# Convolution taps shared anew between VectorE (in PSUM) and TensorE, and seven norms in column form

## The reference

```python
def rmsnorm(x, g):
    y = x * lax.rsqrt(jnp.mean(x * x, axis=-1, keepdims=True) + EPS)
    return y * g

def conformer_conv_module(u, w_pw1, b_pw1, dw_w, dw_b, ln_g, ln_b, w_pw2, b_pw2):
    h = u @ w_pw1 + b_pw1                       # 1024 -> 2048
    a, g = jnp.split(h, 2, axis=-1)
    h = a * jax.nn.sigmoid(g)
    h = causal_depthwise_conv(h, dw_w, dw_b)    # 31 taps per channel
    h = jax.nn.silu(layernorm(h, ln_g, ln_b))
    return h @ w_pw2 + b_pw2
```

## Time and profile before

| | |
|---|---|
| median of 3 runs | 3100.71 us (3097.72 to 3105.9) |
| profiled execution, its own time | 3102.5 us |
| its span, first to last instruction | 3100.7 us |
| mean granted TensorE clock | 0.918 |
| busy: PE, DVE, ACT, POOL | 89%, 48%, 34%, 35% |
| stretch of the convolution taps | 2448.8 to 2644.0 us |
| norms with a reciprocal of 128 x 512 ahead of the product | n0, n1, n2, n3, n4, n6, n8 |

### The profile page before, as it was taken

How to read it: one execution, slowest core, us unless ns; L and a number is a source line. 1 busy time by engine, 2 the same in 40 slices (tenths; PEclk the granted TensorE clock), 3 DMA queues, 4 the chain that set the end, 5 groups by cost and what they waited for, 6 DMA issues and landing times.

```text
span 3100.7 us, 34247 instructions
## 1 busy us (share of the span) xinstructions
PE 2766.6 (89%) x12475; PEld 2225.4 (72%) x12475; DVE 1487.5 (48%) x2187; ACT 1050.2 (34%) x1661; POOL 1100.6 (35%) x551
## 2 busy tenths in 40 slices
PE   3985689899998888999989999999999867799997
PEld 2764457777787667888878888788888644588886
DVE  7499772555414773322133566433321599533312
ACT  2221532322223573333223555433322200433321
POOL 1321001334443222445424455444444322144442
PEclk6897657999999998999979999999999988899998
DMA  6431040355423101223221221122223210122221
GB/s 212 136 109 55 1 136 28 102 161 163 139 95 86 41 28 55 95 95 100 93 61 60 69 64 60 67 95 97 95 92 99 82 41 27 41 95 95 95 95 55
DMA packets 277692, 264.47 MB, mean 85 GB/s; under 512 B 23020, under 2 KB 276557, under 8 KB 277581
## 3 DMA queue, kind: packets, MB, share of 16 engines
q1 hardware_dynamic: 277581, 262.97, 26.6%
HBM read 260.85 MB, written 2.10 MB: 85 GB/s over the span
## 4 chain that ended last, share of the span: by engine, by line
PE 66%; DVE 19%; issue 7%; ACT 2%; DMA 2%; POOL 2%; SPq 1%; DVEq 0%; POOLq 0%; ACTq 0%
PE bank L1153 16%; PE bank L1155 16%; PE bank L1154 16%; DVE v_cm L2182 6%; DVE ada_acc L2347 2%; POOL w_lo L805 2%; DMA root<-in_ada_w_dram 2%; PE bank L893 1%; PE bank L895 1%; PE bank L894 1%; PE bank L1491 1%; DVE root L2353 1%; DVE score L2530 1%; PE bank L1422 1%; PE bank L915 1%
## 5 line engine op out<-in xcount | busy, mean ns | idle before, releaser
L805 POOL TENSOR_TENSOR w_lo<-w_raw,w_hi 128x1024 fp32r<-128x1024 f32 (+1 forms) x364 | 867.7, 2393 | 1651.9 <-ACT w_hi L1740 1079.8
L1153 PE MATMUL bank<-h_hi,w_hi 128*128 128x512 f32 x1632 | 650.6, 399 | 75.7 <-DVE u_pad L2189 30.3
L1154 PE MATMUL bank<-h_lo,w_hi 128*128 128x512 f32 x1632 | 645.0, 395 | 0.0
L1155 PE MATMUL bank<-h_hi,w_lo 128*128 128x512 f32 x1632 | 644.3, 395 | 0.0
L1740 ACT ACTIVATE w_hi<-w_raw 128x1024 fp32r<-128x1024 f32 (+1 forms) x232 | 232.6, 1015 | 588.2 <-PE bank L1155 514.9
L1153 PEld LDWEIGHTS bank<-h_hi,w_hi 128*128 128x128 f32 x1632 | 312.8, 192 | 148.2 <-issue 47.6
L1154 PEld LDWEIGHTS bank<-h_lo,w_hi 128*128 128x128 f32 x1632 | 313.1, 192 | 66.4 <-issue 1.2
L1155 PEld LDWEIGHTS bank<-h_hi,w_lo 128*128 128x128 f32 x1632 | 312.5, 191 | 67.1
L1153 PE MATMUL bank<-a_hi,w_hi 128*128 128x512 f32 x704 | 273.9, 389 | 0.0
L1154 PE MATMUL bank<-a_lo,w_hi 128*128 128x512 f32 x704 | 273.9, 389 | 0.0
L1155 PE MATMUL bank<-a_hi,w_lo 128*128 128x512 f32 x704 | 273.9, 389 | 0.0
(11 more groups left out here) (343 smaller groups left out, 4596.0 us busy)
## 6 DMA issues: line engine op xcount, KB each, us to landing
ada_w<-in_ada_w_dram SPq DMA_DIRECT2D x60, 512.0 KB, 6.0
w_raw<-in_ffn_gate_dram SPq DMA_DIRECT2D x22, 1024.0 KB, 5.1
w_raw<-in_ffn_up_dram SPq DMA_DIRECT2D x22, 1024.0 KB, 5.2
w_raw<-in_ffn_w_gate_dram SPq DMA_DIRECT2D x22, 1024.0 KB, 5.2
w_raw<-in_ffn_w_up_dram SPq DMA_DIRECT2D x22, 1024.0 KB, 5.1
root<-in_ada_w_dram SPq DMA_DIRECT2D x144, 128.0 KB, 2.8
w_raw<-in_ffn_down_dram SPq DMA_DIRECT2D x16, 1024.0 KB, 5.1
w_raw<-in_ssm_w_in_dram SPq DMA_DIRECT2D x16, 1024.0 KB, 5.2
```

Source lines behind the costliest of these rows:

```text
L805: pool.tensor_tensor(w_lo[parity][:, 0:nk, half], w_raw[parity][:, 0:nk, half], w_hi[parity][:, 0:nk, half].bitcast(F32), ALU.subtract).th ...
L1153: pe.matmul(dst[m][:], hi, src_hi(k0 + k), start=first and k == 0, stop=False)
L1154: pe.matmul(dst[m][:], hi, src_lo(k0 + k), start=False, stop=False)
L1155: ins = pe.matmul(dst[m][:], lo, src_hi(k0 + k), start=False, stop=last and k == nk - 1)
```

## The change

- `PE_TAPS` becomes a list by chunk, 9, 9, 9, 9, 9, 10, 14, 15: 84 taps on PE instead of 64.
- `own_taps` accumulates in PSUM bank 5 instead of `v_cm`; the last tap writes `v_cm`.
- DVE's order: the `u_pad` of the next pair come between the two chunks of a pair instead of behind them.
- The diagonals go from POOL (`root`) to ACT (`tap_diag`, two buffers of 16), one activation of 128 x 128 for each tap; ACT does those of chunks c and c+1 behind the sigmoid of each odd c.
- The mean's products (`mean_part`) are spread between slots and taps on PE.
- Norms n0 to n4, n6 and n8: the sums are made with the data as the stationary operand and one column of ones as the moving one, so that bank 4 holds 128 x 4 numbers; the root and the reciprocal work on 128 x 4 (`norm_col`); `spread` on PE multiplies the broadcast column by the identity, so that the factor stands in all rows of bank 4 again, and DVE reads it there in L2309.

```diff
@@ constants and buffers
-PE_TAPS = 8
+PE_TAPS = [9, 9, 9, 9, 9, 10, 14, 15]
+        norm_col = place("norm_col", [P, NT])
+        tap_diag = [in_big(f"tap_diag{j}", [P, 16, P], 72 + 8 * j) for j in range(2)]
@@ gpsimd: tap_diagonals(c) and its calls at m = 3..9 are taken out
@@ cv_pe
             def conv_taps(c):
                 pe.wait_ge(glu_done, c + 1)
-                pe.wait_ge(diag_ready, 2 * c + 2)
+                pe.wait_ge(diag_ready, c + 1)
                 take(6 + c % 2, taps_done, c + 1)
-                for k in range(PE_TAPS):
-                    ins = pe.matmul(bank[6 + c % 2][:], root[k // 4][:, P * (k % 4):P * (k % 4) + P], u_pad[:, c, k:k + S],
+                for k in range(PE_TAPS[c]):
+                    ins = pe.matmul(bank[6 + c % 2][:], tap_diag[c % 2][:, k, :], u_pad[:, c, k:k + S],
...
+            def mean_part(c):
+                if c == 0:
+                    take(4, centred, DC)
+                pe.wait_ge(taps_done, c + 1)
+                ins = pe.matmul(bank[4][:], ones[:], v_cm[:, c, :], start=c == 0, stop=c == DC - 1)
...
                     if 2 * j + q >= 2:
                         conv_taps(2 * j + q - 2)
+                    if 2 * j + q >= 5:
+                        mean_part(2 * j + q - 5)
             conv_taps(6)
+            mean_part(3)
             conv_taps(7)
-            (mean of all 8 chunks here)
+            for c in range(4, DC):
+                mean_part(c)
@@ norm_sums, spread (called behind every norm_sums but those of norms 5 and 7)
                 pe.wait_ge(x_squared, DC * nn + DC)
-                pe.matmul(bank[4][:], ones[:], sq[1][:], start=False, stop=True).then_inc(x_sq_summed, 1)
+                for i in range(NT):
+                    tok = slice(P * i, P * i + P)
+                    pe.matmul(bank[4][:, i:i + 1], tmp[0][:, tok], ones[:, 0:1], start=True, stop=False)
+                    ins = pe.matmul(bank[4][:, i:i + 1], sq[1][:, tok], ones[:, 0:1], start=False, stop=True)
+                ins.then_inc(x_sq_summed, 1)
+            def spread(nn):
+                pe.wait_ge(rinv_ready, ROOT_BASE[f"n{nn}"] + 1)
+                take(4, h_scaled, H_BASE[nn] + DC)
+                for i in range(NT):
+                    ins = pe.matmul(bank[4][:, P * i:P * i + P], norm_col[:, i:i + 1].to_broadcast([P, P]), ident[:],
+                                    start=True, stop=True)
+                ins.then_inc(rinv_spread, 1)
@@ scalar: rms writes norm_col from bank[4][:, 0:NT]; in the convolution stage
+                def diagonals(c):
+                    if c >= 2:
+                        act.wait_ge(pe_taps_done, c - 1)
+                    for k in range(PE_TAPS[c]):
+                        ins = act.activation(tap_diag[c % 2][:, k, :], ident[:], ACT.Copy, scale=col("dw_w", DC * k + c))
+                    ins.then_inc(diag_ready, 1)
+                diagonals(0)
...
+                    if c % 2 == 1:
+                        diagonals(c)
+                        if c + 1 < DC:
+                            diagonals(c + 1)
@@ cv_dve
+                k0 = PE_TAPS[c]
+                acc = bank[5]
+                link(dve.tensor_scalar(acc[:], u_pad[:, c, k0:k0 + S], tap(k0), col("cv_dw_b", c), ALU.mult, ALU.add))
+                for k in range(k0 + 1, TAPS):
+                    link(dve.scalar_tensor_tensor(out=acc[:] if k < TAPS - 1 else v, in0=u_pad[:, c, k:k + S], scalar=tap(k),
+                                                  in1=acc[:], op0=ALU.mult, op1=ALU.add))
...
+            glu_pair(0)
+            for j in range(DC // 2):
+                own_taps(2 * j)
+                if j + 1 < DC // 2:
+                    glu_pair(j + 1)
+                own_taps(2 * j + 1)
@@ vector
+            def rinv_cols(nn):
+                dve.wait_ge(root_done, r + 1)
+                dve.reciprocal(norm_col[:], norm_col[:]).then_inc(rinv_ready, 1)
+                dve.wait_ge(rinv_spread, SPREAD[nn] + 1)
+                return bank[4]
```

More of the change, by code:

```diff
@@ L298, in build @@
         rinv_ready = sem("rinv_ready")
+        rinv_spread = sem("rinv_spread")
         h_scaled = sem("h_scaled")
@@ L806, in low_part @@
                                        w_hi[parity][:, 0:nk, half].bitcast(F32), ALU.subtract).then_inc(w_split, 1)
[L808 to L815, removed]
             n = 0
@@ L1242, in _ @@
             ada_sums(ADA_FIRST)
+            spread(0)
             def later_rows():
@@ L1319, in out_project @@
                     norm_sums(then_norm)
+                    spread(then_norm)
             def swiglu(f, nh, then_norm):
@@ L1776, in rms @@
                 r = ROOT_BASE[name]
-                act.activation(root[r % 2][:], bank[4][:], ACT.Sqrt, bias=eps_col[eps][:], scale=1.0 / width
+                in_cols = name[0] == "n" and int(name[1]) in SPREAD
+                act.activation(norm_col[:] if in_cols else root[r % 2][:], bank[4][:, 0:NT] if in_cols else bank[4][:], ACT.Sqrt, bias=eps_col[eps][:], scale=1.0 / width
                                ).then_inc(root_done, 1)
@@ L2179, in own_taps, with glu_pair @@
                 tap = lambda k: cols[:, ROWS["dw_w"] + DC * k + c:ROWS["dw_w"] + DC * k + c + 1]
[L2180 to L2183, removed]
+                k0 = PE_TAPS[c]
[4 more added lines that the diff above has]
+                                                  in1=acc[:], op0=ALU.mult, op1=ALU.add))
                 dve.wait_ge(pe_taps_done, c + 1)
                 dve.tensor_tensor(v, bank[6 + c % 2][:], v, ALU.add).then_inc(taps_done, 1)
[L2187 to L2194, removed]
+            def glu_pair(j):
+                for c in (2 * j, 2 * j + 1):
+                    dve.wait_ge(sig_done, c + 1)
+                    dve.scalar_tensor_tensor(out=u_pad[:, c, pad:pad + S], in0=bank[c % 2][:], scalar=col("cv_b_pw1", c),
+                                             in1=tmp[c % 2][:], op0=ALU.add, op1=ALU.mult).then_inc(glu_done, 1)
+                dve.wait_ge(glu_done, 2 * j + 2)
+            glu_pair(0)
[4 more added lines that the diff above has]
+                own_taps(2 * j + 1)
             dve.wait_ge(mean_summed, 1)
```

31 lines of the change are left out of this document (14 added, 17 removed).

## The result

The changed kernel takes 3061.03 us (median of 4 runs, 3058.12 to 3064.34) against 3102.9 us for the kernel before in runs beside them (4 runs, 3097.72 to 3105.9): a ratio of 0.987, with a 95% interval of 0.9858 to 0.9882. That is 41.9 us less; the steps of the prediction came to 52.7. Its profiled execution took 3064.34 us, with a span of 3062.3.

A forecast was written before the change was run, and what follows sets the result against it. VectorE was taken to bound the convolution's tap stretch; 36.6 us there plus 16.1 from seven norms made 52.7 us less, 3048 us for the median against 3100.7 before, with 3042 to 3056 at 0.60 and a range of 3036 to 3062.

The forecast's parts named there:

- What bounds the kernel: Convolution tap stretch: VectorE is the bound, busy 183.9 of 195.2 us, with taps held 36.5 us beside GpSimd's work.
- Part 1: Convolution taps on VectorE: accumulating in PSUM, a tap takes 0.786 us with no hold, a chunk's first tap 0.84.
- Rival 1: Convolution taps: GpSimd still holds VectorE despite the PSUM accumulator, 17 us back, 3065; chance 0.05.
- Rival 2: Convolution taps: PSUM taps are dearer by up to 0.1 us, 10 us back at 0.1, 3058; chance 0.13.
- Rival 3: Convolution taps: write and read back of one PSUM bank are serial, a tap 1.57 us, 3151; chance 0.04.
- Part 2: Convolution stage: the new order played through on both engines, last addition at 2607.3 instead of 2643.95, 36.6 us less.
- edits taken at nothing: Convolution stage: 84 diagonals on ScalarE at 0.31 us each and seven mean parts on TensorE were priced at no cost.
- Part 3: Seven norms in column form: 2.5 us less in each of six, 1.1 in n0, in sum 16.1 us.
- Sum 3.6, so 2.5 us less: Norm n6, first sum to first scale: 3.6 us after against 6.10 before.
- what fills them is light, so I leave the clock as it was: Norms: TensorE's idle times get shorter, filled with light work; its clock was assumed to fall as before.
- Rival 4: Norms: they give nothing, since small products run at half clock, 3064; chance 0.05.
- Rival 5: Clock stays full across the norms (1.4 us less in n1, n2, n3, n6), or taps slightly shorter: 3041; chance 0.13.

The follow-up runs named there:

- experiment 3: Kernel before with only VectorE's taps accumulating in PSUM bank 5; old shares, order and GpSimd diagonals: 3070.48 us, ratio 0.9895.
- experiment 5: Changed kernel with VectorE's taps accumulating in v_cm in SBUF again: 3075.61 us, ratio 0.9908 to the kernel before.
- experiment 6: Changed kernel with VectorE's old order, both chunks of a pair before the next pair's gates: 3059.52 us, ratio 0.9855 to the kernel before.
- experiment 1: Changed kernel without any edit of the norms, so the convolution's part alone: 3067.75 us, ratio 0.9886 to the kernel before.
- experiment 2: Kernel before with only the seven norms in column form, convolution stage as before: 3100.78 us, ratio 0.9985.
- experiment 4: Changed kernel with dense filler products nobody reads in six norms (all but n0): 3050.68 us, ratio 0.9834 to the kernel before.
- experiment 8: Kernel before with seven dense filler products of 512 columns behind the sums in n1 to n4 and n6: 3096.26 us, ratio 0.9977.
- tenth experiment: Changed kernel with fillers in six norms, old VectorE order and PE_TAPS 8, 9, 8, 9, 8, 8, 14, 15: 3034.64 us, ratio 0.9782 to the kernel before.

## Why the prediction was right in one part and wrong in the other

**What bounds the kernel, and Part 1: right.** The held time of 36.5 us was real, and its cause was the accumulator's place (experiments 3 and 5). Of a tap with its hand-over, priced at 0.786 us, 20 take 15.79 us, 0.79 each. The first tap of a chunk, priced at 0.84, is 0.81 + 0.03. Rivals 1, 2 and 3 (holds stay, taps up to 0.1 dearer, write and read back serial) are refuted by one line, 754/756/756. The rule on VectorE's fixed cost from PSUM ("VectorE: DVE Perf Modes" of the Trainium skill, section on the TRN2 errata), by which a tap would have been 65 ns longer, is not borne out: the difference is 4 ns. The other rule ("SBUF — State Buffer" of the Trainium skill, section Who interferes with whom), that a VectorE instruction with two SBUF inputs contends with GpSimd's reads and one with a single SBUF input, outside the 2-port modes, does not, held also with the result written to PSUM (a longest tap of 756 ns).

**Part 2: right.** The schedule gave 36.6 us; measured is 36.6. While it waits for the second pair's gates, VectorE was to run no tap for 11.8 us (2474.5 to 2486.3), and ran none for 11.6 (2473.54 to 2485.18). The last addition ended at 2606.19 instead of near 2594 since the norms ahead, which were to give 13.6 us, had brought the first gate only 1.2 us forward. The edits taken at nothing (84 diagonals on ScalarE, mean parts on TensorE) cost nothing that shows, although a diagonal took 0.39 us instead of the 0.31 of the price. What I didn't draw out of my own numbers is how little the 20 taps moved off VectorE could pay: they are 15.7 us less work for it, but it then stands waiting for TensorE for 11.6 us in the new order and for 10.8 in the old one (experiment 6).

**Part 3: wrong, and the step that failed is "Sum 3.6, so 2.5 us less", together with "what fills them is light, so I leave the clock as it was".** The term of spread was sized 1.0 us, with rows at full clock; it measured 2.08 in all of the six but n2 (1.84). The sums' 1.85 held in n2 and n6 (1.9), but in n1, n3 and n4 they took 3.0 to 3.1, and 2.9 in n8. Root, reciprocal and the scale's read from PSUM (0.74 us) were sized right, and the hop to TensorE ahead of the spread, taken at 0.15, was 0.05. In n6 the terms make 1.91 + 0.52 + 0.05 + 2.08 + 0.03 = 4.6 us from the first sum to the first scale, not 3.6. In place of 2.5 us each, the six norms gave 0.25 to 1.67 us, and n0 gave 0.6 for 1.1. The mistake was in the reading of the earlier trace rows: they showed when the clock fell behind 2 us of dense sums, and I carried that time over to sums that take as long and do little. My bound for that step at half clock (6.3 us) described n1, at 5.7 from first sum to scale, better than the value that I took. Rival 4, to which I gave 0.05, had the right mechanism and nearly the right time, 3064; I argued against it with L935's 0.11 us a row, a row at full clock inside busy work, which says what a row costs at that clock and not whether it keeps it. Experiments 1 and 2 put the loss in the norms, and 4 and 8 show it to be the clock: fillers give 10.4 us after and 8.7 before. Rival 5 (the clock stays full) was the other way round, but its price of 1.4 us a norm is what experiment 8 shows in n6: its first gate, at 2438.07, is 17.4 us behind the first product, 1.4 less than 18.9.

What stays open: why the fall comes at different points of like sums (after two or three pairs in n1, n3, n4 and n8, behind all eight in n2 and n6), and at another point for the same norm in another version; how the 8.7 us of experiment 8 divide over its five norms; and what sets the two groups in the tenth experiment's runs.

## What to carry to other kernels

A chain of VectorE instructions with two inputs in SBUF beside a working GpSimd: move the accumulator to a free PSUM bank before re-sharing any work. When a short chain of small TensorE products takes the place of dense ones, price each of them at both clocks, and charge the dense work behind it too; then try dense products that nobody reads in the idle time. After a bound is relieved, play both engines through the window before moving work from one to the other: the busy times alone don't say who waits for whom.

## What the runs showed of the hardware that was not expected

- An accumulation in PSUM, read and written by each of 20 VectorE instructions of 128x512 float32 in a row, costs 756 ns each against 752 in SBUF. The first of a chunk, with one input only, is 810 ns to PSUM against 545 to SBUF (the kernel before):

```profile
L2180 DVE TENSOR_SCALAR v_cm<-u_pad,cols x8: 536/545/547, 2455.0 to 2625.4; 128x512 f32<-128x512 f32 x8
```

- Sixteen one-column rows in a row, each with its weight load, take 1.9 us at 2.4 GHz. In n1 the clock fell during them (0.95 in the us from 558, 0.50 in the one from 559), though TensorE is shown busy for the whole of the second. Before, n1's two dense sums were followed by 2.2 us of idle TensorE at full clock, up to 559. A TensorE that the page shows busy was not enough to keep 2.4 GHz.
- One GpSimd low part held a two-input SBUF tap by about 2.0 us (experiment 5: 24.50 against 16.51 us beside four of them), and GpSimd's own builds took 1490 ns instead of 1051 in the same contention.
- Work that computes nothing made both kernels faster, by 10.4 and 8.7 us by the medians.
